# Linear layers issued as 256-column matmuls in a two-block mixer kernel on one core

## Chip, core and metric

The kernel runs on one core of one Trainium2 chip. The metric is the device time of one execution in microseconds; the kernel is run several times and the median is taken. TensorE multiplies (its weight loads are listed as PEld, its matmuls as PE), VectorE is DVE, ScalarE is ACT, GpSimd is POOL and SyncE is SP.

## What is computed

One sequence of 512 tokens with 1024 features goes through four layers. Two layers of a first block mix retention, a state-space scan and a forgetting attention; a second block has an RWKV layer and a dilated-attention layer, each with a memory attention over 256 memory tokens and with two gated feed-forward networks. Nearly all multiplications are in the linear layers:

```
def _layer(x, c, positions, norm_g, w_ada, b_ada, w_in, ...):
    h = _rmsnorm(x, norm_g) * (1.0 + scale[:, None, :]) + shift[:, None, :]
    proj = h @ w_in
    ...
    out = mixed @ w_out
    return x + gate[:, None, :] * out

def swiglu_ffn(x, norm_g, w_in, w_out):
    gate, up = jnp.split(rms_norm(x, norm_g) @ w_in, 2, axis=-1)
    return (jax.nn.silu(gate) * up) @ w_out

def memory_attention(q, mem, mem_norm_g, w_kv, q_gain, k_gain):
    k, v = jnp.split(rms_norm(mem, mem_norm_g) @ w_kv, 2, axis=-1)
    ...

x = x + 0.5 * swiglu_ffn(...)        # twice in each layer of the second block
y = jnp.concatenate([y_main, y_mem], axis=-1) @ a_w_out[i]
x = x + y
```

All of it is float32.

## The kernel before

Features lie on the 128 partitions and the 512 tokens on the free axis, so a linear layer is a list of pieces: a piece is the weight block that gives 128 output features, with k_tiles (8, in some pieces 6 or 4) blocks of 128 input features. A piece arrives by one DMA into `raw` (a ring of four buffers), ScalarE rounds it into `w_hi` (line 379), and VectorE subtracts to get the rest, `w_lo` (line 386). Both have two buffers. The operand, too, is a pair `hi`, `lo`. A product is then three matmuls for each k, all summed in one PSUM bank of 512 float32 columns: `w_hi*hi`, `w_hi*lo`, `w_lo*hi`. A piece of eight blocks has 24 matmuls. The type of both operands is float32r.

`Linear` walks over all pieces of the whole program. `Segment` says for a stretch of pieces what the moving operand is, how many columns it has (`n`, 512 nearly everywhere), and which reader takes the bank away. Only the two segments `keys(0)` and `keys(1)`, eight pieces in all, multiply the 256 memory tokens and have n = 256, with moving slices at column 0 and at column 256 of the same tile:

```
        return Segment(4, tuple(x[:, :, i * MEM:(i + 1) * MEM] for x in parts),
                       Scaled(dst, prep.r, prep.ready), n=MEM, ready=lambda k: prep.operand_ready(i, k))
```

On every engine the stages are woven into one instruction stream by planned times (`weave`); `step` in `Linear` is the planned time of three matmuls, and it isn't touched by the change. On TensorE the matmuls of other stages (attention, scans) stand between the k blocks of a piece. TensorE waits at the start of a piece for `split_done` (w_lo made) and for the bank to be free. ScalarE may round piece g + 2 when all matmuls of piece g are done (`tile_done`), and VectorE follows it.

Of the kernel before, what the change touches and what calls it, by code (L numbers as in the profile page):

```python
# [17 lines left out]
T = 512  # L18
# [3 lines left out]
DEPTH = 2  # L22
KC = 8
RING = 4

RET_HEADS = 4
SSD_HEADS, SSD_DIM = 16, 64
# [207 lines left out]
class Stage:  # L235
# [5 lines left out]
    def pe(self, pe):  # L241
        return ()
# [11 lines left out]
class Core:  # L254


    def __init__(self, nc, ctx, dram):
# [4 lines left out]
        self.piece = 0  # L262
        self.raw = [self.sb(f"raw{s}", [P, KC, P]) for s in range(RING)]
        self.w_hi = [self.sb(f"w_hi{s}", [P, KC, P], F32R) for s in range(2)]
        self.w_lo = [self.sb(f"w_lo{s}", [P, KC, P], F32R) for s in range(2)]
        self.const = self.sb("const", [P, CONST_ARRAY.shape[1]])
        self.vec = self.sb("vec", [P, NVEC])
        self.acc = [ctx.enter_context(nc.psum_tensor(f"acc{s}", [P, T], F32)) for s in range(RING)]
        self.aux = [ctx.enter_context(nc.psum_tensor(f"aux{s}", [P, T], F32)) for s in range(4)]

        self.weights_ready = [self.sig(f"weights_ready{s}") for s in range(RING)]
        self.split_hi = self.sig("split_hi")
# [97 lines left out]
    def load_piece(self, sp, g):  # L370
        tensor, at, k = self.stream[g]
        dst = self.raw[g % RING][:, 0:k, :].rearrange("p k m -> p (k m)")
        sp.dma_start(dst, self.dram[tensor][at]).then_inc(self.weights_ready[g % RING].handle, 16)

    def split_piece_hi(self, act, g):

        s, k = g % RING, self.stream[g][2]
        act.wait_ge(self.weights_ready[s].handle, 16 * (g // RING + 1))
# [26 lines left out]
class Linear(Stage):  # L405
# [51 lines left out]
    def pe(self, pe):  # L457
        def matmuls():
            core = self.core
            for s, u, g, k_tiles, start, _, step in self.tiles:  # L460
                yield start
                if u == 0 and s.after:
                    pe.wait_ge(*s.after())
                pe.wait_ge(core.split_done.handle, g + 1)
                if self.banks[g - self.first][1]:
                    pe.wait_ge(*self.banks[g - self.first][1])
                hi, lo = s.moving
                w_hi, w_lo = core.w_hi[g % 2], core.w_lo[g % 2]
                for k in range(k_tiles):
                    if k:  # L470
                        yield start + k * step
                    if s.ready and u == 0:
                        pe.wait_ge(*s.ready(k))
                    for q, (w, a) in enumerate(((w_hi, hi), (w_hi, lo), (w_lo, hi))):
                        mm = pe.matmul(self.bank(s, g), w[:, k, :], a[:, k, 0:s.n],  # L475
                                       start=(k == 0 and q == 0), stop=(k == k_tiles - 1 and q == 2))
                    if s.release and u == s.count - 1 and k < k_tiles - 1:
                        mm.then_inc(*s.release.inc())
                mm.then_inc(core.tile_done.handle, 1)
        return (matmuls(),)  # L480
# [1029 lines left out]
class Attention(Stage):  # L1510
# [3 lines left out]
    at, ready = None, ()  # L1514
# [1336 lines left out]
class HeadNorms(Stage):  # L2851


    at = None
# [1219 lines left out]
```

## Time and profile before

| | us |
|---|---|
| median of 3 runs | 3478.35 (3477.93 to 3479.72) |
| span of the profiled execution | 3482.5 |
| TensorE busy with matmuls | 3349.0 (96% of the span) |
| TensorE busy with weight loads | 2599.3 (75%) |
| VectorE busy | 1780.3 (51%) |
| ScalarE busy | 1196.0 (34%) |
| GpSimd busy | 409.8 (12%) |

The span of the profiled execution is its own time; it lies 4.1 us above the median of the runs. Matmuls are pipelined: a record's duration runs from its start to a modelled end, and the next one starts before that end. What a matmul costs in a row of them is the distance from one start to the next. A weight load overlaps with the matmul before it.

### The profile page before, as it was taken

The page shows a single profiled execution, that of the slowest core. Times are in us where ns is not written, and L with a number is a line of the kernel's source. Part 1 is how long each engine was busy: PE and PEld are TensorE (multiplying, and loading weights), DVE is VectorE, ACT ScalarE, POOL GpSimd, SP SyncE. Part 2 cuts the span into 40 slices and gives each one's busy share as a digit, 9 for nine tenths or more (in the row PEclk, how much of TensorE's full clock was granted, in tenths as well). Part 3 has the DMA queues.
Part 4 walks back from the last instruction along what each step waited for, and adds up shares of the span by engine and source line. Part 5 has one row for each costly group of instructions (what it writes and reads, how often), then busy time and mean ns, then how long its engine had stood idle before and what let it go on. Part 6 is the DMA issues. An engine that isn't in the chain of part 4 may idle for free.

```text
span 3482.5 us, 44013 instructions
## 1 busy us (share of the span) xinstructions
PE 3349.0 (96%) x18330; PEld 2599.3 (75%) x18330; DVE 1780.3 (51%) x2532; ACT 1196.0 (34%) x1884; POOL 409.8 (12%) x318
## 2 busy tenths in 40 slices
PE   5999999899999899999999999999999999999999
PEld 4766678576677788887777777888777887678887
DVE  6854454744436743336767554434454335463433
ACT  3344432433443422224333242222353224342221
POOL 0000011000000311002322111100101011011110
PEclk8999999999999999999999999999999999899999
DMA  5631123221222333333200014332322332013332
GB/s 208 212 110 62 51 97 96 67 85 55 61 80 81 101 92 96 93 97 109 68 14 2 26 51 123 92 97 85 102 80 86 96 89 90 10 61 97 91 97 85
DMA packets 83909, 295.44 MB, mean 85 GB/s; under 512 B 9472, under 2 KB 12800, under 8 KB 81664
## 3 DMA queue, kind: packets, MB, share of 16 engines
q1 hardware_dynamic: 78384, 270.61, 25.3%
q10 hardware_dynamic: 5328, 22.02, 1.9%
q8 instruction: 146, 2.39, 0.3%
q14 instruction: 51, 0.42, 0.0%
HBM read 283.94 MB, written 8.65 MB: 84 GB/s over the span
## 4 chain that ended last, share of the span: by engine, by line
PE 83%; DVE 8%; ACT 2%; issue 1%; POOL 1%; DMA 1%; DVEq 0%; POOLq 0%; ACTq 0%
PE acc L475 66%; PE acc L1464 1%; DVE w_lo L386 1%; PE acc L3217 1%; PE acc L2443 1%; DVE square_sums L2902 1%; PE aux L3181 1%; PE aux L1745 1%; PE aux L3186 1%; PE acc L1776 1%; DMA late_ada<-in_ada 1%; ACT w_hi L379 1%; DVE ssd_ex L1366 1%; PE acc L2447 1%; PE acc L2433 1%
## 5 line engine op out<-in xcount | busy, mean ns | idle before, releaser
L475 PE MATMUL acc<-op_hi,w_hi 128*128 128x512 f32 x2624 | 1100.4, 419 | 37.1 <-DVE w_lo L386 16.6
L475 PE MATMUL acc<-op_lo,w_hi 128*128 128x512 f32 x2624 | 1041.7, 397 | 0.0
L475 PE MATMUL acc<-op_hi,w_lo 128*128 128x512 f32 x2624 | 1040.9, 397 | 0.0
L379 ACT ACTIVATE w_hi<-raw 128x1024 fp32r<-128x1024 f32 (+2 forms) x476 | 494.7, 1039 | 1581.6 <-PE acc L475 1549.6
L386 DVE TENSOR_TENSOR w_lo<-raw,w_hi 128x1024 fp32r<-128x1024 f32 (+2 forms) x476 | 576.6, 1212 | 288.5 <-ACT w_hi L379 288.1
L475 PEld LDWEIGHTS acc<-op_hi,w_hi 128*128 128x128 f32 x2624 | 495.9, 189 | 219.2 <-issue 82.4
L475 PEld LDWEIGHTS acc<-op_hi,w_lo 128*128 128x128 f32 x2624 | 496.0, 189 | 120.3
L475 PEld LDWEIGHTS acc<-op_lo,w_hi 128*128 128x128 f32 x2624 | 496.8, 189 | 115.5 <-issue 11.5
L475 PE MATMUL acc<-ffn_hi,w_hi 128*128 128x512 f32 x800 | 316.5, 396 | 0.0
L475 PE MATMUL acc<-ffn_lo,w_hi 128*128 128x512 f32 x800 | 316.1, 395 | 0.0
L475 PE MATMUL acc<-ffn_hi,w_lo 128*128 128x512 f32 x800 | 316.1, 395 | 0.0
L594 DVE SCALAR_TENSOR_TENSOR x<-acc,x 128x512 f32<-128x512 f32 x112 | 77.4, 691 | 286.8 <-PE acc L475 286.7
L815 POOL TENSOR_TENSOR ffn_gate<-ffn_gate,rstd 128x512 f32<-128x512 f32 x66 | 114.8, 1740 | 836.5 <-ACT ffn_gate L806 836.5
L795 DVE TENSOR_TENSOR ffn_product<-ffn_gate,acc 128x512 f32<-128x512 f32 x88 | 60.4, 686 | 260.3 <-PE acc L475 256.1
L475 PEld LDWEIGHTS acc<-ffn_lo,w_hi 128*128 128x128 f32 x800 | 150.2, 188 | 36.8 <-issue 0.2
L475 PEld LDWEIGHTS acc<-ffn_hi,w_hi 128*128 128x128 f32 x800 | 150.2, 188 | 36.6 <-issue 0.2
L475 PEld LDWEIGHTS acc<-ffn_hi,w_lo 128*128 128x128 f32 x800 | 150.2, 188 | 36.4
L790 DVE TENSOR_TENSOR ffn_gate<-acc,rstd 128x512 f32<-128x512 f32 x66 | 45.6, 691 | 183.9 <-PE acc L475 183.8
L1264 ACT ACTIVATE ssd_ex<-aux,ssd_ncum 128x512 f32<-128x512 f32 (+3 forms) x128 | 62.4, 522 | 85.9 <-PE aux L1450 85.9
L1366 DVE TENSOR_TENSOR ssd_ex<-ssd_ex,ssd_cb 128x1024 f32<-128x1024 f32 (+1 forms) x64 | 60.2, 949 | 47.2 <-ACT ssd_ex L1264 47.1
L815 POOL TENSOR_TENSOR ffn_gate<-ffn_gate,square_sums 128x512 f32<-128x512 f32 x22 | 40.0, 1816 | 275.4 <-ACT ffn_gate L806 275.4
L653 POOL TENSOR_TENSOR square_sums<-square_sums,squares 128x512 f32<-128x512 f32 x35 | 56.2, 1604 | 95.9 <-ACT squares L632 95.9
(578 smaller groups left out, 3901.6 us busy)
## 6 DMA issues: line engine op xcount, KB each, us to landing
raw<-in_w SPq DMA_DIRECT2D x436, 512.0 KB, 3.6
late_ada<-in_ada ACTq DMA_DIRECT2D x32, 512.0 KB, 4.4
raw<-in_w SPq DMA_DIRECT2D x32, 384.0 KB, 3.0
ada<-in_ada ACTq DMA_DIRECT2D x4, 1024.0 KB, 15.0
ada<-in_ada SPq DMA_DIRECT2D x4, 1024.0 KB, 21.9
x_mid<-x SPq DMA_DIRECT2D x16, 256.0 KB, 3.4
x<-x_mid SPq DMA_DIRECT2D x2, 2048.0 KB, 9.1
skew<-rel_rows SPq DMA_DIRECT2D x12, 192.0 KB, 3.0
```

Source lines behind the costliest of these rows:

```text
L379: act.activation(self.w_hi[g % 2][:, 0:k, :], self.raw[s][:, 0:k, :], ACT.Copy).then_inc(self.split_hi.handle, 1)
L386: dve.tensor_tensor(self.w_lo[g % 2][:, 0:k, :], self.raw[g % RING][:, 0:k, :], self.w_hi[g % 2][:, 0:k, :].bitcast(F32), ALU.subtract).th ...
L475: mm = pe.matmul(self.bank(s, g), w[:, k, :], a[:, k, 0:s.n], start=(k == 0 and q == 0), stop=(k == k_tiles - 1 and q == 2))
L594: dve.scalar_tensor_tensor(out=x[:, u, :], in0=bank, scalar=self.scale(u), in1=x[:, u, :], op0=ALU.mult, op1=ALU.add).then_inc(core.freed[ ...
L653: pool.tensor_tensor(core.ss[i][:, :], core.ss[i][:, :], src, ALU.add).then_inc(*self.summed.inc())
L790: dve.tensor_tensor(f.gate[:, slot, :], bank, f.rstd, ALU.mult).then_inc(freed, 1)
L795: dve.tensor_tensor(f.product[:, slot, :], f.gate[:, slot, :], bank, ALU.mult).then_inc(freed, 1)
L815: pool.tensor_tensor(f.gate[:, q % 2, :], f.gate[:, q % 2, :], f.rstd, ALU.mult).then_inc(*f.gated.inc())
L1264: act.activation(self.ex[u % self.EX][:, e, 0:n], core.aux[2 * (u % 2) + e][:, 0:n], ACT.Exp, bias=self.ncum[:, b, 2 * pair + e:2 * pair + ...
L1366: dve.tensor_tensor(ex, ex, tiled(cb[pair // 4][:, at[b]:at[b] + n], 2), ALU.mult).then_inc(*self.weighted.inc())
L1464: mm = pe.matmul(core.acc[2 + pair % 2][e * HD:(e + 1) * HD, b * P:T], self.xdt[:, b, h * SSD_DIM:(h + 1) * SSD_DIM], self.ex[u % self.EX] ...
L1745: pe.matmul(core.aux[e][:, 0:n], self.q[half[e], j, t * P:n], self.k[half[e], j, 0:n], start=True, stop=False, skip_group_check=True)
```

## The change

Each matmul of a linear layer is issued as two, over columns 0 to 255 and 256 to 511 of the moving operand, into the same columns of the bank, with the same weights. The segments with n = 256 keep one matmul. Flags, waits and signals stay at the first or the last matmul of the group.

```
+STREAM = T // 2
...
-                hi, lo = s.moving
+                (hi, lo), bank = s.moving, self.bank(s, g)
                 w_hi, w_lo = core.w_hi[g % 2], core.w_lo[g % 2]
                 for k in range(k_tiles):
...
                     for q, (w, a) in enumerate(((w_hi, hi), (w_hi, lo), (w_lo, hi))):
-                        mm = pe.matmul(self.bank(s, g), w[:, k, :], a[:, k, 0:s.n],
-                                       start=(k == 0 and q == 0), stop=(k == k_tiles - 1 and q == 2))
+                        for at in range(0, s.n, STREAM):
+                            mm = pe.matmul(bank[:, at:at + STREAM], w[:, k, :], a[:, k, at:at + STREAM],
+                                           start=(k == 0 and q == 0 and at == 0),
+                                           stop=(k == k_tiles - 1 and q == 2 and at + STREAM == s.n))
```

TensorE's stream, at the end of a layer of the first block, where the sum of squares for the next norm (aux) stands between two segments. Before:

```order
L475 MATMUL acc<-out_hi,w_hi 128x512
L475 MATMUL acc<-out_lo,w_hi 128x512
L475 MATMUL acc<-out_hi,w_lo 128x512
L678 MATMUL aux<-square_sums,const 128x512
L475 MATMUL acc<-op_hi,w_hi 128x512
L475 MATMUL acc<-op_lo,w_hi 128x512
```

The same place with the change:

```order
L477 MATMUL acc<-out_hi,w_hi 128x256 x2
L477 MATMUL acc<-out_lo,w_hi 128x256 x2
L477 MATMUL acc<-out_hi,w_lo 128x256 x2
L681 MATMUL aux<-square_sums,const 128x512
L477 MATMUL acc<-op_hi,w_hi 128x256 x2
L477 MATMUL acc<-op_lo,w_hi 128x256 x2
```

Nothing moved: each of the 10,944 matmuls of 512 columns at line 475 became two neighbours at line 477, the 192 matmuls of 256 columns (keys) stayed as they were, and all other instructions of TensorE and of the other engines keep their order.

## Rows read from the trace of the kernel before

**Rows 1.** The page: span, busy times, and TensorE's granted clock in 40 slices

```profile
span 3482.5 us, 44013 instructions
PE 3349.0 (96%) x18330; PEld 2599.3 (75%) x18330; DVE 1780.3 (51%) x2532; ACT 1196.0 (34%) x1884; POOL 409.8 (12%) x318
PEclk8999999999999999999999999999999999899999
```

**Rows 2.** The page: the chain that ended last, by engine and line

```profile
PE 83%; DVE 8%; ACT 2%; issue 1%; POOL 1%; DMA 1%; DVEq 0%; POOLq 0%; ACTq 0%
PE acc L475 66%; PE acc L1464 1%; DVE w_lo L386 1%; PE acc L3217 1%; PE acc L2443 1%; DVE square_sums L2902 1%; PE aux L3181 1%; PE aux L1745 1%; PE aux L3186 1%; PE acc L1776 1%; DMA late_ada<-in_ada 1%; ACT w_hi L379 1%; DVE ssd_ex L1366 1%; PE acc L2447 1%; PE acc L2433 1%
```

**Rows 3.** The chain's own view: shares, then start us, us, what; the long pieces

```profile
by line: PE acc L475 65.6%; issue 1.5%; PE acc L1464 1.3%; DVE w_lo L386 1.3%; PE acc L3217 0.8%; PE acc L2443 0.7%; DVE square_sums L2902 0.7%; PE aux L3181 0.7%; PE aux L1745 0.6%; PE aux L3186 0.6%; PE acc L1776 0.6%; DMA late_ada<-in_ad
...
1206.53 379.72 PE acc L475 x1650
...
2037.30 46.46 PE acc L475 x198
...
2152.58 309.40 PE acc L475 x1326
2463.09 76.30 PE acc L475 x327
...
2638.43 279.30 PE acc L475 x1197
...
3114.34 364.95 PE acc L475 x1563
```

**Rows 4.** The chain in time, window 260 to 300 us, a mixed stretch

```profile
261.20 2.99 PE acc L475 x12
264.59 0.80 PE acc L1464 x4
...
274.92 1.14 DVE w_lo L386
276.05 2.24 DVE ssd_ex L1366
```

**Rows 5.** TensorE's timeline in a feed-forward network: start us, us, operands, shape

```profile
1352.29 0.39 PE L475 MATMUL acc<-op_hi,w_hi 128*128 128x512 f32 x1
1352.52 0.39 PE L475 MATMUL acc<-op_lo,w_hi 128*128 128x512 f32 x1
...
1357.65 0.39 PE L475 MATMUL acc<-op_hi,w_lo 128*128 128x512 f32 x1
```

**Rows 6.** The timeline in keys, first half: 256-column matmuls, one weight load

```profile
1179.62 0.28 PE L475 MATMUL acc<-mem_hi,w_hi 128*128 128x256 f32 x1
...
1182.23 0.28 PE L475 MATMUL acc<-mem_hi,w_lo 128*128 128x256 f32 x1
...
1191.86 0.28 PE L475 MATMUL acc<-mem_hi,w_hi 128*128 128x256 f32 x1
1191.86 0.19 PEld L475 LDWEIGHTS acc<-mem_lo,w_hi 128*128 128x128 f32 x1
1191.97 0.28 PE L475 MATMUL acc<-mem_lo,w_hi 128*128 128x256 f32 x1
...
1197.19 0.28 PE L475 MATMUL acc<-mem_hi,w_lo 128*128 128x256 f32 x1
```

**Rows 7.** The timeline at the end of keys, up to the next segment

```profile
1206.53 0.39 PE L475 MATMUL acc<-mem_hi,w_hi 128*128 128x256 f32 x1 [0.84 <-DVE w_lo L386]
...
1206.87 0.28 PE L475 MATMUL acc<-mem_hi,w_lo 128*128 128x256 f32 x1
...
1212.17 0.28 PE L475 MATMUL acc<-mem_hi,w_lo 128*128 128x256 f32 x1
```

**Rows 8.** The timeline where the clock was low, 512 and 256 columns

```profile
1166.69 0.63 PE L475 MATMUL acc<-out_hi,w_hi 128*128 128x512 f32 x1
...
1168.83 0.63 PE L475 MATMUL acc<-out_hi,w_lo 128*128 128x512 f32 x1
...
1201.57 0.41 PE L475 MATMUL acc<-mem_hi,w_lo 128*128 128x256 f32 x1
...
1204.35 0.41 PE L475 MATMUL acc<-mem_hi,w_hi 128*128 128x256 f32 x1
```

**Rows 9.** The timeline of ScalarE and VectorE: the split of one piece

```profile
1352.49 1.06 ACT L379 ACTIVATE w_hi<-raw 128x1024 fp32r<-128x1024 f32 x1 [4.02 <-PE acc L475]
...
1353.58 1.23 DVE L386 TENSOR_TENSOR w_lo<-raw,w_hi 128x1024 fp32r<-128x1024 f32 x1 [0.40 <-ACT w_hi L379]
```

**Rows 10.** A window of the RWKV stage: us, busy (records) by engine, clock

```profile
1790.00:1830.00 40.00, 39.06 (x687) 32.49 (x684) 27.70 (x67) 15.71 (x29) 10.50 (x15) 1.00 0.01 2
```

**Rows 11.** The page: the queues that fetch instructions

```profile
q8 instruction: 146, 2.39, 0.3%
q14 instruction: 51, 0.42, 0.0%
```

## The prediction

> **What bounds the kernel now.** I read the page first, for who is busy and whether TensorE's clock is low: TensorE has matmuls in flight for 96% of the span, the next engine for 51%, and the granted clock is near full in almost every slice [rows 1]. A busy TensorE isn't yet a bound, so the chain that ended last comes next: 83% of it is TensorE, and 66% is one line, 475, the matmuls of the linear layers [rows 2]; the chain's own view has 65.6% [rows 3]. In order of time the chain shows six long pieces of that line alone, 379.72 + 46.46 + 309.40 + 76.30 + 279.30 + 364.95 = 1456 us together [rows 3], with nothing of another engine in them: there each nanosecond per matmul counts in full. The rest of the line's share, 0.656 x 3482.5 = 2284 us less 1456, so 828 us, lies in mixed stretches, where pieces of 12 matmuls (2.99 us) alternate with the scan's matmuls and now and then with VectorE [rows 4].
>
> Then the question is what one matmul costs. Durations don't tell (0.39 us each, with the next begun after 0.23), so I take starts. In a feed-forward network the 24 matmuls of a piece start from 1352.29 to 1357.65 us: 5.36 us over 23 steps, **233 ns** [rows 5]; the long chain pieces say the same, 309.40 / 1326 = 233.3 ns and 279.30 / 1197 = 233.3 ns [rows 3].
>
> **What the change does, and its price.** It removes 10,944 matmuls of 512 columns and adds 21,888 of 256, each with its own weight load, since in the trace every matmul has one, with as many weight loads as matmuls on the page [rows 1]. Nothing else changes place. So the price is twice the step of a 256-column matmul with a fresh weight load, less 233.3 ns.
>
> That very instruction is in the trace, in the memory keys. It has the same types, the same 128x128 load, moving slices at column 0 and at column 256. It has two steps there:
> - From 1191.86 to 1197.19 us, two pieces back to back without a wait, 48 matmuls: 5.33 us over 47 steps, **113.4 ns** [rows 6]. Two of them are 226.8 ns, 6.5 ns less than one of 512.
> - From 1206.87 to 1212.17 us, 45 steps in 5.30 us: **117.8 ns** [rows 7]. Two are 235.6 ns, 2.3 ns more than one of 512.
>
> Both have the full clock, and both hold over a piece boundary. Of the eight pieces of the keys, five run at the quick step (the first of them from 1179.62 to 1182.23 us, 23 steps, 113.5 ns [rows 6]), the sixth falls mostly into low clock [rows 8], and the last two are the slow ones. The first matmuls after a wait are irregular; of five such starts one settled at the slow step. I don't see in the rows what chooses. Bank and weight buffers recur in both, and so do both moving slices (the quick stretch runs from the last piece of the first slice into the second). Note what the rows say of a fixed cost per matmul: if a step were a fixed part plus columns, 233.3 - 113.4 = 119.9 ns for 256 columns would make the fixed part 113.4 - 119.9, less than nothing. So a 512-column matmul pays something in its second half that a 256-column one doesn't pay; I can't name it, only price it.
>
> What is on the path: 2284 us less about 22 us of keys (192 x 113.4 ns, at most) are 2262 us of 512-column matmuls, / 233.3 ns = 9,700 of them. In the long pieces they are about 1456 / 0.2333 = 6,240, in the mixed stretches 3,460.
> - Long pieces at the quick step: 6,240 x 6.5 ns = 41 us.
> - Mixed stretches: 3,460 x 6.5 ns = 22 us if all of it counted. The neighbours there are other engines' results [rows 4], which don't come sooner, so I count four fifths: 18 us.
> - Low clock: at half clock (1.2 GHz) 512 columns step 2.14 us / 5 = 428 ns and 256 columns 2.78 us / 13 = 214 ns [rows 8], exactly half, so there the change is worth nothing. The granted clock is at 0.9 or more in all but two slices [rows 1]; I take 1 us off.
>
> Sum: 41 + 18 - 1 = 58 us. The profiled execution's own time is its span, 3482.5 us, so 3424.5 for it; it stood 4.1 us above the median of the runs, so the median becomes 3478.35 - 58 = **3420 us**.
>
> What could need cover and has it: the split of the next piece but one. ScalarE begins at 1352.49, when a piece has ended, and VectorE ends at 1353.58 + 1.23 = 1354.81 us [rows 9], while TensorE needs it only when the next piece is over, one piece (24 x 233.3 ns = 5.6 us) later, at about 1358. A piece becomes 24 x 6.5 = 156 ns shorter, of 3.1 us of slack. In the keys, where a piece lasts 2.7 us, this cover is gone and TensorE waits 0.84 us for w_lo [rows 7]; that is far from 5.4 us.
>
> Instructions: the trace has 44,013 of them for 2.39 + 0.42 MB fetched, 64 bytes each [rows 1, 11]. 21,888 more records (10,944 matmuls and 10,944 loads) are 1.4 MB more over 3.4 ms. TensorE's queue must deliver one load and one matmul each 113 ns. In the RWKV stage it delivers 687 matmuls with 684 loads in 40 us, one pair each 58 ns [rows 10]. So supply shouldn't bind.
>
> A rule of the notes speaks against the change. The steps above say that a matmul has no positive fixed part: 233.3 ns against 2 x 113.4 [rows 5, 6]. The Trainium skill (TensorE: Matmul & The Clock Gate, Back-to-back issue gap) has a warm gap of N / 2.4 + 2.5 ns. By that rule one of 512 takes 215.8 ns and two of 256 take 218.3, 2.5 ns more for each pair, an estimate of 24 us more for 9,700. This case's trace disagrees on both sizes (233.3 and 113.4 or 117.8); the order of the two is right only in the slow step.
>
> **Rivals.**
> 1. *A mixture.* Both steps occur, as in the keys, where five pieces of seven at full clock, 0.7, are quick: 0.7 x 6.5 - 0.3 x 2.3 = 3.9 ns per pair, x 9,700 = 38 us, less a fifth of the mixed part: about 3445 us. For it: each wait or mixed stretch is a new start, and one start of five in the keys went slow. Against it: the long pieces run 300 us unbroken, so a few starts decide most, and the 512-column step is the same 233.3 ns in all of them.
> 2. *A fixed cost per matmul, the other side.* The doubled number of weight loads holds the 256-column step at the slow 117.8 ns for good. Place: everywhere in line 475; price: 2.3 ns x 9,700 = 22 us, so 3500 us. It decides from a step above 233.3 / 2 = 116.7 ns on. For it: rows 7 shows it lasting for 45 steps, after which the segment ended; it is also the side on which the rule above falls (24 us, by the page alone). Against it: the quick step held longer in total. And the new stream has something that the keys have not: the same weights loaded twice in a row, and the two halves of a bank in turn. Neither is in a row; by the nearest ones their price lies between the two steps.
> 3. *Nothing to be seen.* The quick step comes, but what follows on VectorE, or half slow and half quick steps, eats it: within 7 us of 3478. At an even mixture the gain is still 2.1 ns per pair, 20 us; zero takes three slow steps of four (0.26 x 6.5 = 0.74 x 2.3). Unlikely as an exact balance.
> 4. *Supply.* If TensorE's queue can't hold one pair per 113 ns when weights stream in by DMA as well, each step grows. The stage of rows 10 had a DMA share of only 0.01, so this isn't excluded; at 124 ns, say, 14.7 ns per pair x 9,700 gives 143 us more, 3620 us.
>
> **How the numbers follow.** Quick step nearly everywhere 0.53 (3412 to 3432 us: all of the mixed part counted, or none of it and some slow steps); mixture 0.21 (3432 to 3470); nothing 0.07; slow step 0.15 (3485 to 3503); supply 0.04. A gain beyond the quick step would need a step under 113 ns; the low clock's 214 ns for 256 columns would be 107 at full clock, so it is possible in principle, but no row at full clock shows it, and I leave a little room below. The range goes from 3406 to 3488 us: it leaves out most of the slow case and supply. The likeliest case alone has 3412 to 3432. 0.2% is 7 us, about what a measurement of this kernel can tell from no change. Faster: 0.53 + 0.21 = 0.74; the same 0.07; slower 0.15 + 0.04 = 0.19.
>
> **What the changed profile would show.** Right: starts in a feed-forward network 113.4 ns apart, a piece of 24 products in 5.44 us instead of 5.60, as many weight loads as matmuls (29,274 each), the last long piece of the chain about 355 us instead of 365, and no new wait for w_lo in it. Wrong in size: steps of 117 to 118 ns, or both kinds in turns. Wrong in kind: steps well above 118 ns with TensorE's queue as the releaser, or matmuls without a load of their own and a step under 113 ns. A step that depends on which half of the bank or which of two equal loads it is would also be new, since the keys can't show it.

## The result and the profile after

The changed kernel takes 3452.02 us (median of 4 runs, 3450.12 to 3457.01), the one before 3479.03 (3477.93 to 3481.28). The ratio is 0.9928, with a 95% interval of 0.9914 to 0.9943: **27 us faster**, where 58 were forecast. The page of the kernel after, its span, busy times, clock, instruction queue and chain:

```profile
span 3451.6 us, 65901 instructions
...
PE 3316.5 (96%) x29274; PEld 3098.3 (90%) x29274; DVE 1779.5 (52%) x2532; ACT 1196.0 (35%) x1884; POOL 409.6 (12%) x318
...
PEclk8999999999999999999999999999999999989999
...
q8 instruction: 231, 3.78, 0.4%
...
PE 83%; DVE 9%; ACT 2%; issue 2%; POOL 1%; DMA 0%; DVEq 0%; POOLq 0%; ACTq 0%
```

The counts are as worked out: 29,274 matmuls and as many weight loads, and 1.39 MB more of instructions. Against [rows 1, 2] the shares of the chain hardly moved, the clock not at all. Weight loads are now in flight for 90% of the span, and in the long stretches all the time. The windows view of four of them has, by column, us, busy and count of PE and of PEld, then DVE, ACT, POOL, clock and DMA:

```profile
1199.00:1563.00 364.00, 364.00 (x3211) 364.00 (x3212) 153.45 (x177) 104.02 (x129) 49.87 (x29) 1.00 0.33 103
2131.00:2442.00 311.00, 311.00 (x2643) 311.00 (x2642) 128.88 (x147) 90.00 (x114) 40.61 (x24) 1.00 0.30 94
2620.00:2900.00 280.00, 280.00 (x2380) 280.00 (x2379) 111.67 (x127) 77.78 (x97) 36.76 (x22) 1.00 0.30 93
3094.00:3448.00 354.00, 354.00 (x3121) 353.94 (x3120) 141.67 (x157) 94.59 (x113) 39.21 (x22) 1.00 0.31 95
```

Divide time by matmuls: 113.4, 117.7, 117.6 and 113.4 ns. Two stretches run at the quick step of [rows 6], two at the slow one of [rows 7], from end to end. TensorE's timeline inside the first and the second shows the same (each row now is two neighbours, one product):

```profile
1299.99 0.39 PE L477 MATMUL acc<-op_lo,w_hi 128*128 128x256 f32 x2
...
1305.65 0.39 PE L477 MATMUL acc<-op_hi,w_lo 128*128 128x256 f32 x2
...
2200.01 0.40 PE L477 MATMUL acc<-op_hi,w_hi 128*128 128x256 f32 x2
...
2205.66 0.40 PE L477 MATMUL acc<-op_hi,w_hi 128*128 128x256 f32 x2
```

5.66 us over 25 products is 226.4 ns, 5.65 us over 24 is 235.4 ns. And the long pieces of the chain, the counterpart of [rows 3]:

```profile
1199.00 364.77 PE acc L477 x3216
...
2016.45 45.17 PE acc L477 x396
...
2130.21 312.34 PE acc L477 x2652
2443.62 77.03 PE acc L477 x654
...
2619.32 281.96 PE acc L477 x2394
3093.57 354.88 PE acc L477 x3126
```

For the same products, half as many as the matmuls here, the last stretch went from 364.95 to 354.88 us (10.1 less), and 46.46 became 45.17. But 309.40 became 312.34, 76.30 became 77.03 and 279.30 became 281.96: 6.3 us more together. The first holds other matmuls than in [rows 3] (1,608 products against 1,650 matmuls, some of them keys); at 6.5 ns for each of about 1,600 it gave 10.4, an estimate. So the long stretches gave 10.1 + 1.3 + 10.4 - 6.3 = 15.5 us of the 30.9 by which the span fell. The other 15.4 us are a remainder: the mixed stretches, and with them all by which one execution differs from another.

### The profile page after: what moved, and what is told of

It is laid out like the page before. It is cut to its first block, busy times and chain, and to the rows that moved or that the text cites. A ratio compares the mean times of both kernels' runs of the same rounds, so it can differ in the third digit from the quotient of the medians.

```text
span 3451.6 us, 65901 instructions
## 1 busy us (share of the span) xinstructions
PE 3316.5 (96%) x29274; PEld 3098.3 (90%) x29274; DVE 1779.5 (52%) x2532; ACT 1196.0 (35%) x1884; POOL 409.6 (12%) x318
## 4 chain that ended last, share of the span: by engine, by line
PE 83%; DVE 9%; ACT 2%; issue 2%; POOL 1%; DMA 0%; DVEq 0%; POOLq 0%; ACTq 0%
PE acc L477 65%; DVE w_lo L387 1%; PE acc L1467 1%; PE acc L3220 1%; PE acc L2446 1%; ACT w_hi L380 1%; DVE square_sums L2905 1%; PE aux L1748 1%; PE aux L3184 1%; PE acc L1779 1%; DVE ssd_ex L1369 1%; PE acc L2450 1%; PE acc L2436 1%; PE aux L3189 1%; PE aux L1766 1%
## 5 line engine op out<-in xcount | busy, mean ns | idle before, releaser
L477 PE MATMUL acc<-op_hi,w_hi 128*128 128x256 f32 x5248 | 1096.8, 291 | 36.6 <-DVE w_lo L387 16.8
L477 PE MATMUL acc<-op_lo,w_hi 128*128 128x256 f32 x5248 | 1036.3, 279 | 0.0
L477 PE MATMUL acc<-op_hi,w_lo 128*128 128x256 f32 x5248 | 1034.6, 279 | 0.0
L477 PEld LDWEIGHTS acc<-op_hi,w_hi 128*128 128x128 f32 x5248 | 805.4, 190 | 123.2 <-issue 90.6
L477 PEld LDWEIGHTS acc<-op_lo,w_hi 128*128 128x128 f32 x5248 | 802.6, 189 | 0.0
L477 PEld LDWEIGHTS acc<-op_hi,w_lo 128*128 128x128 f32 x5248 | 799.1, 189 | 0.0
L477 PE MATMUL acc<-ffn_hi,w_hi 128*128 128x256 f32 x1600 | 316.2, 279 | 0.0
L477 PE MATMUL acc<-ffn_lo,w_hi 128*128 128x256 f32 x1600 | 315.7, 279 | 0.0
L477 PE MATMUL acc<-ffn_hi,w_lo 128*128 128x256 f32 x1600 | 315.6, 279 | 0.0
L477 PEld LDWEIGHTS acc<-ffn_lo,w_hi 128*128 128x128 f32 x1600 | 244.2, 189 | 0.0
```

The source lines that it names most:

```text
L477: mm = pe.matmul(bank[:, at:at + STREAM], w[:, k, :], a[:, k, at:at + STREAM], start=(k == 0 and q == 0 and at == 0), stop=(k == k_tiles - ...
```

## The experiments

Where a share of quick steps is given below, it is counted over all steps from one 256-column matmul to the next in the run's trace that are 112 to 115 ns (quick) or 116 to 120 ns (slow). A series is a row of such matmuls with no matmul of another stage between them. The kernels up to the uneven first product have one time each, beside one of before on the same chip (3471.89 us); the later ones have several.

**The changed kernel again, twice.** No edit.

> The changed kernel once more, unaltered. In its first profile the long unbroken stretches of linear layers ran either at a step of 113.3 ns per 256-column matmul or at 117.8 ns, each stretch at one of them from end to end. Theory P (the step is chosen by chance when a stretch is entered): the same stretches come out with other steps than in the first profile, at least one of the four longest differs in one of two repeats. Theory A (it is chosen by addresses or by the program's order): every stretch has the same step as before, the four longest again quick, slow, slow, quick.

> The same kernel a second time. Theory P: again another pattern of quick and slow stretches, and a span that moves with it (each of the four longest stretches is worth 12 to 14 us between its two steps). Theory A: the same pattern and a span within 3 us of the first.

Measured 3436.51 and 3450.45 us. Three of the four longest pieces in the chain of the first repeat (the one that begins near 1200 us is left out), and then of the second:

```profile
2132.36 291.76 PE acc L477 x2574
...
2609.72 267.27 PE acc L477 x2358
3076.28 354.89 PE acc L477 x3126
```

```profile
2143.95 312.34 PE acc L477 x2652
...
2632.81 271.34 PE acc L477 x2394
3090.35 354.90 PE acc L477 x3126
```

291.76 / 2574 is 113.3 ns, 312.34 / 2652 is 117.8: the same stretch of the same program, quick once and slow once. In the second repeat the stretch that begins near 1200 us is slow, in the first profile it was quick. The quick share is 0.56 in the first profile, 0.78 and 0.51 in these two. Theory A is out for the long stretches: neither an address nor the program's order alone chooses their step.

The four traces of the changed kernel (the fourth comes below) show more. In 158 stretches of 40 steps or more in which every step is 112 to 120 ns, 65,716 steps in all, the state never changes after its first dozen steps. But not every entry is a toss. Matched by their place in the program, 244 series of 12 matmuls or more end in the quick state in all four traces in 154 cases and in the slow one in 34 (two of these are fairly long, 474 and 372 matmuls); 56 differ, or are mixed in one trace. These 56 hold about three quarters of the steps, and the five longest series are among them. So the place in the program does weigh in most short series, and theory P holds where the time is.

Where a series of 13 matmuls or more begins behind another stage's matmul, its first step often tells what will follow: first steps of 205 to 207 ns led to the quick state 64 times of 64, those of 220 to 224 ns 381 times and to the slow one 12 times, those of 225 and 226 ns to the slow one 45 times of 45. But 90 series began with 200 to 203 ns, and there it tells nothing: 47 became quick and 43 slow. Of the 80 such series with 40 steps or more, 42 began so.

**Many widths.** The loop goes over one of eight patterns, by piece:

```
+WIDTHS = ((512,), (256, 256), (384, 128), (320, 192), (288, 224), (128,) * 4, (192, 192, 128), (272, 240))
...
+def widths(n, g):
+    return (n,) if n < T else WIDTHS[(g + g // 8) % 8]
...
+                        for width in widths(s.n, g):
```

> Each 512-column product is cut by one of eight patterns, changing from piece to piece: 512; 256+256; 384+128; 320+192; 288+224; four of 128; 192+192+128; 272+240. It gives the step of each width with a fresh weight load behind it. Theory L (below some width the weight load sets the step): widths 128, 192 and 224 all step at 107 to 113 ns, and 256 is the widest that is free, so every other pattern is slower than 256+256: 384+128 about 175 + 109 = 284 ns, four of 128 about 436 ns. Theory C (columns set the step, plus a small fixed part): 128 columns step near 60 ns and all patterns lie within 10 ns of 233. By L the whole kernel is about 200 to 400 us slower than before, by C within 1%.

4031.45 us, 560 more than before. TensorE's timeline, one row a product (the shape is that of its first matmul); for each pattern two rows of one piece:

```profile
1519.90 0.39 PE L482 MATMUL acc<-op_lo,w_hi 128*128 128x256 f32 x2
...
1522.16 0.39 PE L482 MATMUL acc<-op_hi,w_lo 128*128 128x256 f32 x2
...
1522.62 0.45 PE L482 MATMUL acc<-op_lo,w_hi 128*128 128x384 f32 x2
...
1527.18 0.45 PE L482 MATMUL acc<-op_hi,w_lo 128*128 128x384 f32 x2
...
1535.80 0.61 PE L482 MATMUL acc<-op_lo,w_hi 128*128 128x128 f32 x4
1536.25 0.61 PE L482 MATMUL acc<-op_hi,w_lo 128*128 128x128 f32 x4
...
1550.10 0.50 PE L482 MATMUL acc<-op_hi,w_hi 128*128 128x192 f32 x3
...
1553.78 0.50 PE L482 MATMUL acc<-op_hi,w_lo 128*128 128x192 f32 x3
...
1554.64 0.40 PE L482 MATMUL acc<-op_hi,w_lo 128*128 128x272 f32 x2
...
1559.67 0.40 PE L482 MATMUL acc<-op_hi,w_lo 128*128 128x272 f32 x2
...
1560.14 0.39 PE L482 MATMUL acc<-op_lo,w_hi 128*128 128x512 f32 x1
...
1565.28 0.39 PE L482 MATMUL acc<-op_hi,w_lo 128*128 128x512 f32 x1
```

A product then takes, by these rows (steps from product to product in brackets): 256+256 226 ns (10), 512 234 (22), 272+240 240 (21), 384+128 285 (16), 192+192+128 335 (11), four of 128 450 (1). In the median over all their pieces the last is 445 and 384+128 is 282.5. The two other patterns, whose rows aren't shown, take 247 (288+224) and 259 ns (320+192) in the median. The finest cut shows a floor: 445 / 4 = 111 ns for a matmul of 128 columns, which has but a quarter of the columns, and 335 / 3 = 112 ns for two of 192 and one of 128. That is theory L, and theory C is out. Half a bank is the only cut of the seven that beats 512 columns.

That the weight load sets the floor, and not the matmul, no edit shows, but the trace of the kernel before does. Line 3217 there has rows of eight 128x128 loads with matmuls of only 64 columns:

```profile
2952.62 1.00 PE L3217 MATMUL aux<-mem_v,late_probs 128*128 128x64 f32 x8
```

Behind the first, their steps are 111 or 112 ns too, as are 137 of the 208 steps of that line. The RWKV stage, with loads of 64x64 for the most part, has a pair each 58 ns [rows 10]. The floor doesn't explain everything: with 111 ns for the 240 columns, 129 are left for 272, which is 16 ns more than 256 columns take. Nor do the single starts of an uneven cut lie as such a split of its sum has it (after the 384 columns mostly 224 to 231 ns, after the 128 mostly 57 to 60), so only the sums are used here.

**Uneven first product.** All products are 256+256, but the first of each piece is (256 + c) + (256 - c).

```
+KICKS = (0, 4, 8, 16, 32, 64, 12, 24)
...
+    c = KICKS[(g + g // 8) % 8] if first else 0
+    return (n,) if n < T else (256 + c, 256 - c)
```

> The changed kernel, but the first product of each piece is cut unevenly, at 256 + c columns with c = 0, 4, 8, 12, 16, 24, 32 or 64 by turns, all others at 256 + 256. Theory P (the step is a state that a disturbance can reset): the state changes at such pieces within the long stretches, which it never did with even cuts, and for some c it goes from slow to quick and not back. Then the share of quick steps is above the 55% or so of the changed kernel. Theory A: each piece keeps the step it had in the changed kernel, and only the first product is longer by about c / 2.4 ns.

3454.63 us, quick share 0.62. TensorE's timeline, the first product of each piece where it is uneven (the shape gives 256 + c; between 1298.59 and 1309.90 stands the piece with c = 0, and the order leaves out 32 there):

```profile
1293.13 0.40 PE L483 MATMUL acc<-op_hi,w_hi 128*128 128x268 f32 x2
...
1298.59 0.40 PE L483 MATMUL acc<-op_hi,w_hi 128*128 128x280 f32 x2
...
1309.90 0.40 PE L483 MATMUL acc<-op_hi,w_hi 128*128 128x260 f32 x2
...
1315.55 0.40 PE L483 MATMUL acc<-op_hi,w_hi 128*128 128x264 f32 x2
...
1321.01 0.40 PE L483 MATMUL acc<-op_hi,w_hi 128*128 128x272 f32 x2
...
1326.48 0.39 PE L483 MATMUL acc<-op_hi,w_hi 128*128 128x320 f32 x2
```

The piece with c = 12 takes 5.46 us (quick). From c = 24 on it is (1309.90 - 1298.59) / 2 = 5.66 us (slow), c = 4 leaves it slow (5.65), c = 8 makes it quick (5.46), c = 16 leaves it so (5.47). Over all uninterrupted pieces, by the state before the uneven product and behind it (kept / all; - where no piece came in slow):

```
c           0    4    8    12   16   24   32   64
quick kept  5/5  6/6  11/11 35/35 29/29 0/33 41/41 38/38
slow kept   29/29 30/31 3/27 -   0/8  -    -    -
```

So the two steps are states. In long series only a disturbance was seen to change them, and 24 columns (10 ns at 2.4 GHz) more in one matmul turned quick into slow each time.

**Reset at every fourth piece, everywhere and in the long stretches alone; and the changed kernel beside them.** Against the kernel with uneven cuts, the first:

```
-    c = KICKS[(g + g // 8) % 8] if first else 0
+    c = 16 if first and g % 4 == 0 else 0
```

> The changed kernel, but the first product of every fourth piece is cut at 272 + 240 columns. In the run with uneven cuts that one left the quick step quick (29 of 29 pieces) and turned the slow one quick (8 of 8). If the two steps are states that are entered by chance and cost what they seem to, nearly every 256-column step in the long stretches is 113.3 ns now, the four longest stretches are all quick, and the time is near what was predicted at first with the quick step everywhere: about 58 us below before, less some 3 us for the uneven products, so a ratio of 0.983 to 0.986. Rival: the reset only shuffles, the share of quick steps stays near 0.5 to 0.8, and the ratio is 0.990 to 0.993 as for the changed kernel.

The second leaves the 512-column matmul in all pieces outside the long stretches:

```
+    long = 141 <= g <= 243 or 256 <= g <= 325 or 341 <= g <= 391 or g > 400
+    return (n,) if n < T or not long else (256 + c, 256 - c)
```

> As the kernel with 272 + 240 columns at every fourth piece, but products are cut only in pieces 141 to 243, 256 to 325, 341 to 391 and from 401 on, which hold the long unbroken stretches; in all other pieces (mixed stretches) the 512-column matmul stays. If mixed stretches give back four fifths of their quick step's 22 us, this kernel is some 12 to 18 us slower than the one that cuts everywhere. If they give nothing (starts after waits are irregular there, and neighbours set the time), both are equal within 4 us.

> The changed kernel unaltered, timed beside the others. By the chance-state theory its single times scatter over 10 to 40 us, several times the scatter of before, between about 0.983 and 1.000 of before, and the median is near 0.991.

| kernel | median us | ratio to before (95%) | quick share in its profile |
|---|---|---|---|
| 272+240 at every fourth piece | 3426.78 (3423.99 to 3433.31) | 0.9866 (0.9849 to 0.9883) | 0.83 |
| the same, long stretches alone | 3436.40 (3429.64 to 3453.78) | 0.9891 (0.9874 to 0.9907) | 0.93 of those that are cut |
| changed kernel unaltered | 3452.26 (3423.56 to 3457.69) | 0.9925 (0.9897 to 0.9953) | 0.49 |

Before had 3473.94 us beside them, in 17 runs from 3465.8 to 3484.47. So the reset works: about 47 us less than before, and 25 less than the changed kernel, by one uneven product in four pieces. Its median is the lowest of the study. The expected ratio of 0.983 to 0.986 is just missed. Of the slow 17% that are left, five sixths are in series of less than 350 matmuls, where 0.61 of the steps are quick against 0.96 in longer ones: each interruption is a new entry. The last stretch of the chain in this kernel, and in the changed kernel beside it, where it was slow:

```profile
3063.67 355.32 PE acc L482 x3126
```

```profile
3083.79 368.33 PE acc L477 x3126
```

(368.33 - 355.32) us / 3126 = 4.2 ns per matmul; the uneven products' own cost is already paid in it. The unaltered kernel scatters over 34 us with one run at 3423.56, as by chance states; but before itself scattered over 19 us here, more than the 3 us of its four runs in the result, so the scatter alone proves little. The scatter of before goes with the granted clock (3465.8 us at 0.984, 3481.8 at 0.978). The states don't: of the two repeats above, the quicker had a clock of 0.978 and the slower one of 0.983. Cutting the mixed stretches is worth 3436.4 - 3426.8 = 10 us, less than the 12 to 18 expected, and the intervals overlap.

**The slow state on purpose.** c = 24 in place of 16.

> As the kernel with 272 + 240 columns, but the cut at every fourth piece is 280 + 232. In the run with uneven cuts that one turned the quick step slow in 33 of 33 pieces. If slow stays slow there (not seen yet), the long stretches run at 117.8 ns throughout, and the kernel is slower than before by up to 22 us, the fixed-cost rival's 3500 us (ratio 1.003 to 1.008). If the cut turns slow into quick as well, groups of four pieces alternate and the ratio is near 0.995. If the state didn't matter, it would be as fast as the others.

3477.74 us in 10 runs, ratio 1.0015 (1.0004 to 1.0026), quick share 0.23. The last stretch of its chain:

```profile
3109.10 368.20 PE acc L482 x3126
```

368.20 / 3126 = 117.8 ns: slow stays slow at this cut, in its trace in 68 uninterrupted pieces of 68, and quick turned slow in 10 of 10. The gain is gone. The kernel lost 4 to 5 us, less than the expected ratio of 1.003 to 1.008, and not the 22 of a kernel that is slow in every step: series of less than 350 matmuls had half of their steps quick still.

**Reset at every piece.**

```
-    c = 16 if first and g % 4 == 0 else 0
+    c = 16 if first else 0
```

> As the kernel with the first product cut at 272 + 240 in every fourth piece, but in every piece. There 17% of the 256-column steps stayed slow, nearly all in mixed stretches. One uneven product costs about 26 ns (355.32 us against 354.89 us for 65 pieces with 17 of them), so 351 more of them cost 9 us at most. If it makes half of the remaining slow steps quick (1,700 x 4.4 ns = 8 us, four fifths of it counted), both nearly cancel: ratio 0.986 to 0.988, not better than every fourth piece. If entries after waits take the step by themselves whatever the first product is, the slow share stays at 17% and the ratio is 0.988 to 0.990.

3429.01 us (3421.16 to 3439.59), ratio 0.9874 (0.9855 to 0.9892), quick share 0.83. The time is what the first branch expected and the share what the second did, so neither is met whole. Split by length, the share rose from 0.61 to 0.71 in series of less than 350 matmuls and fell from 0.96 to 0.90 in longer ones. In the long ones the steps from an uneven product on are 121, 110, 119, 120, 118 and 118 ns before 113 comes back, 26 ns more than six quick steps, which is the uneven product's price. The states themselves hardly moved: series of 12 to 349 matmuls end quick in 161 of 207 cases (0.78) here, in 170 of 227 (0.75) with every fourth piece, and in 0.75 to 0.80 in the four traces of the changed kernel. So the first product does little to decide which state is taken at an entry.

**Halves in turn.** Per block k, the three products of one half of the columns come first, then those of the other half.

```
+                    for half in range(halves):
+                        for q, (w, a) in enumerate(((w_hi, hi), (w_hi, lo), (w_lo, hi))):
+                            cut = sum(widths(s.n, g, k == 0)[:1])
+                            at, width = (cut, s.n - cut) if half else (0, cut)
```

> As the kernel with 272 + 240 at every fourth piece, but for each block k the three products of the first half of the columns come first and then the three of the second half, so that one half of the bank takes three matmuls in turn and w_lo and w_hi alternate otherwise (where the piece is cut unevenly, all three products of its first block are). Theory N (neither equal weights in a row nor the turn of the halves has a price): the steps are the same 113.3 and 117.8 ns, the time is within 6 us of the other kernel. Rival: if a repeated load of equal weights is cheaper or dearer than a new one, or writing the same half again costs, the quick step moves away from 113.3 ns.

3453.90 us (3449.6 to 3462.3), ratio 0.9948 (0.9932 to 0.9964), quick share 0.53, so it missed the 6 us. But the steps are the same: the timeline in a quick piece has

```profile
1339.91 0.28 PE L484 MATMUL acc<-op_lo,w_hi 128*128 128x256 f32 x1
...
1341.73 0.28 PE L484 MATMUL acc<-op_hi,w_lo 128*128 128x256 f32 x1
```

1.82 us over 16 steps, 113.8 ns, and over all steps of the trace the commonest are 113 and 118 ns. What differs is the disturbance, three products cut at 272 + 240 instead of one: through the long stretches it turned quick to slow and slow to quick, by turns, so that four pieces of eight were slow. Theory N holds for the two steps, not for the time, which was lost to the state: with nearly half of the steps slow, 9,700 x (0.53 x 6.5 - 0.47 x 2.3) ns = 23 us were to be gained by the prediction's own prices, and 18 were.

## Why the prediction was wrong

- *What bounds the kernel*: right. Line 475 was the path, and no other wait took its place. The split's cover, the supply of instructions (pairs of load and matmul each 113 ns over 355 us, with weights streaming in at 95 GB/s) and the counts came out as written. Supply as a rival is out.
- *The two prices*: right to a tenth. 113.4 and 117.8 ns were read from eight pieces of the keys, and hold over thousands of steps, whichever half of the bank and whichever of two equal loads it is.
- *The step that failed*: "Quick step nearly everywhere 0.53", and from it "Long pieces at the quick step: 6,240 x 6.5 ns = 41 us". These pieces gave 15.5 us in the profiled run, since three of six ran slow from end to end. The two steps were seen, and what chooses them was said to be unknown. Yet "one start of five in the keys went slow" was taken to favour quick, and the mixture priced as a rival at 5 pieces of 7. Five starts can't bear that: in four traces the shares were 0.56, 0.78, 0.51 and 0.49.
- *The first rival*, the mixture, is what happened. With a share of 0.56, its formula gives 9,700 x (0.56 x 6.5 - 0.44 x 2.3) = 25 us, and 27 were measured; that it lies so near is partly luck, since single runs of the same kernel lay from 16 to 50 us below the median of before in the table. That few starts decide most was right too, but it speaks for scatter, not for the quick step.
- *Mixed stretches*: "I count four fifths: 18 us" was too much as well, for the same reason. Outside the six long pieces 0.58 of the steps were quick in the profiled run, and 3,460 x (0.58 x 6.5 - 0.42 x 2.3) ns is 10 us. About 10 us is also what their cut was worth with the reset. The remainder of 15.4 us in the profiled run is more, but holds the scatter between executions. Whether four fifths of a quicker step come through stays open.
- *A fixed cost per matmul*: not there. The widths show a floor (111 ns with a 128x128 load) instead, which no sum in the prediction had, though the kernel before had rows of it; it would have told that a much finer cut must lose. The steps of 233 ns at 512 columns, 113 at 256 and 111 at 128 don't lie on one line, as a fixed part and a time per column would.
- *The rule that spoke against the change*: the rule N / 2.4 + 2.5 ns of the Trainium skill (TensorE: Matmul & The Clock Gate, Back-to-back issue gap) has 215.8 ns at 512 columns and 55.8 ns at 128; this case's traces have 233 and 111. The Trainium skill gives the rule in that section for a matmul by itself, without a weight load, so it was no forecast for pairs of load and matmul.

Shown by experiment: in the long stretches the state differs from one execution of the same program to the next, lasts until disturbed, costs 4.4 ns per matmul, and can be set. Not settled: what the states are in the hardware, what chooses one at an entry, and why a 512-column matmul takes 233 ns where its columns at 2.4 GHz are 213. No run changed operand placement or the width of the type.

## What to carry to other kernels

Before a matmul is cut in two, read from the trace the step of the smaller one *with its own weight load behind it*, and compare twice that with the larger one's: the load sets a floor (111 ns here for a 128x128 load), so parts whose columns take less than that lose. Measure the cut itself all the same: 272+240 lost too, for a reason that stays open. When a few rows of the same instruction show two different steps, each constant over a series, treat them as states and price the change with both; a few entries of one execution don't give their odds, and repeats of the same kernel do. Then look for a cheap disturbance that sets the good one: here one product of 272 + 240 columns in four pieces was worth about as much again as the change.

## What was not expected of the hardware

- A row of equal matmuls with weight loads locked into one of two steps, 113.3 or 117.8 ns, and held it for up to 3,250 steps; no change in 158 stretches of 40 steps or more, the first dozen of each left out.
- The first step after another stage's matmul foretold the state where it was 205 to 207 ns (quick, 64 of 64), 220 to 224 (quick, 381 of 393) or 225 to 226 (slow, 45 of 45), and not where it was 200 to 203 (47 quick, 43 slow).
- 188 of 244 series ended in the same state in all four executions, most of them short ones; the five longest differed.
- 24 columns more in one matmul turned quick into slow 33 times of 33, 16 columns turned slow into quick 8 times of 8, and 12, 32 or 64 left quick as it was (114 of 114).
- The matmul with 512 columns has no such pair of prices. In the kernel before it has two patterns, 231 and 236 ns in turn or 233, 233 and 234, but in all 12 uninterrupted series of more than 100 steps the mean is 233.3 or 233.4 ns.
